# Squares and sums of the second mixer's norm, moved between the gate slabs of the per-layer embedding

## The reference

```python
for i in range(DEPTH):
    xn = _rms(h, norm_mix[i])
    ...
    h = h + mix.astype(h.dtype)
    h = h + _swiglu(_rms(h, norm_ffn[i]), w_ffn_gate[i], w_ffn_up[i], w_ffn_down[i])
    gate = jax.nn.sigmoid(_rms(h, norm_ple[i]) @ w_ple_gate[i])
    h = h + gate * (p[i] @ w_ple_proj[i])
```

## Time and profile before

| | us |
|---|---|
| median of 3 runs | 2720.02 |
| lowest, highest | 2715.08, 2721.79 |
| the profiled execution | 2719.05 |
| its span | 2716.8 |
| mean granted clock of TensorE | 0.956 of full |

### The profile page before, as it was taken

How to read it: one execution, slowest core, us unless ns; L and a number is a source line. 1 busy time by engine, 2 the same in 40 slices (tenths; PEclk the granted TensorE clock), 3 DMA queues, 4 the chain that set the end, 5 groups by cost and what they waited for, 6 DMA issues and landing times.

```text
span 2716.8 us, 40339 instructions
## 1 busy us (share of the span) xinstructions
PE 2558.7 (94%) x15853; PEld 2183.0 (80%) x15853; DVE 1369.3 (50%) x2136; ACT 1164.1 (43%) x1836; POOL 22.6 (1%) x35
## 2 busy tenths in 40 slices
PE   6999999998999999999999879999889998869998
PEld 4777787875777788777887748998779997848998
DVE  4332334995423233422333575555776666476665
ACT  3332223464433322433222365544565554455554
POOL 0000000000000000000000000000000001000000
PEclk7999999999999999999999898998999998689999
DMA  7444532200344432444322303554335554303553
GB/s 280 182 162 177 199 141 83 103 16 31 139 183 158 184 109 102 149 166 179 122 101 93 124 1 115 180 185 174 109 110 191 180 193 148 129 1 105 180 189 146
DMA packets 52723, 374.85 MB, mean 138 GB/s; under 512 B 5822, under 2 KB 7034, under 8 KB 8736
## 3 DMA queue, kind: packets, MB, share of 16 engines
q1 hardware_dynamic: 50288, 360.73, 36.4%
q0 software_dynamic: 1920, 12.27, 1.3%
q10 hardware_dynamic: 432, 0.73, 0.1%
HBM read 372.55 MB, written 7.39 MB: 140 GB/s over the span
## 4 chain that ended last, share of the span: by engine, by line
PE 87%; DVE 7%; ACT 3%; issue 1%; DMA 1%; SPq 0%; ACTq 0%; DVEq 0%
PE acc L1728 27%; PE acc L1729 26%; PE acc L1730 26%; PE bank L1803 3%; ACT sc L1121 1%; PE bank L1830 1%; DVE sc L1663 1%; DMA ada_raw<-in_slabs 1%; DVE sc L1634 1%; DVE wlo L1208 1%; DVE prod L577 1%; PE Mod L1813 0%; ACT whi L739 0%; PE bank L1851 0%; DVE stt L1656 0%
## 5 line engine op out<-in xcount | busy, mean ns | idle before, releaser
L1208 DVE TENSOR_TENSOR wlo<-raw,whi 128x1024 fp32r<-128x1024 f32 x538 | 651.2, 1223 | 943.0 <-ACT whi L739 942.5
L739 ACT ACTIVATE whi<-raw 128x1024 fp32r<-128x1024 f32 x538 | 559.5, 1055 | 990.0 <-PE acc L1730 929.2
L1728 PE MATMUL acc<-hhi,whi 128*128 128x256 f32 (+1 forms) x2800 | 945.6, 338 | 24.7 <-DVE hlo L1292 11.5
L1729 PE MATMUL acc<-hlo,whi 128*128 128x256 f32 (+1 forms) x2800 | 934.4, 334 | 0.0
L1730 PE MATMUL acc<-hhi,wlo 128*128 128x256 f32 (+1 forms) x2800 | 933.9, 334 | 0.0
L1728 PEld LDWEIGHTS acc<-hhi,whi 128*128 128x128 f32 x2800 | 538.0, 192 | 107.6 <-issue 54.3
L1730 PEld LDWEIGHTS acc<-hhi,wlo 128*128 128x128 f32 x2800 | 537.9, 192 | 50.6
L1729 PEld LDWEIGHTS acc<-hlo,whi 128*128 128x128 f32 x2800 | 538.2, 192 | 48.8 <-issue 0.2
L1728 PE MATMUL acc<-ghi,whi 128*128 128x512 f32 (+1 forms) x1056 | 357.3, 338 | 0.0
L1729 PE MATMUL acc<-glo,whi 128*128 128x512 f32 (+1 forms) x1056 | 357.2, 338 | 0.0
L1730 PE MATMUL acc<-ghi,wlo 128*128 128x512 f32 (+1 forms) x1056 | 357.2, 338 | 0.0
(11 more groups left out here) (261 smaller groups left out, 2370.5 us busy)
## 6 DMA issues: line engine op xcount, KB each, us to landing
raw<-in_slabs SPq DMA_DIRECT2D x333, 1024.0 KB, 4.8
ada_raw<-in_slabs SPq DMA_DIRECT2D x8, 1024.0 KB, 23.2
skew_dram<-lines_dram POOLq DMA_DIRECT2D x1, 6144.0 KB, 24.9
bt<-skew_dram POOLq DMA_DIRECT2D x4, 1024.0 KB, 7.1
x<-in_x_in SPq DMA_DIRECT2D x1, 2048.0 KB, 17.7
out<-x SPq DMA_DIRECT2D x1, 1024.0 KB, 4.8
rope<-in_rope POOLq DMA_DIRECT2D x1, 512.0 KB, 4.4
mask<-in_mask POOLq DMA_DIRECT2D x1, 512.0 KB, 5.3
```

The source lines that it names most:

```text
L739: nc.scalar.activation(whi[:, n % 2, cols], raw_of(n, cols), ACT.Copy).then_inc(ready, 1)
L1208: nc.vector.tensor_tensor(wlo[:, n % 2, cols], raw_of(n, cols), whi[:, n % 2, cols].bitcast(F32), ALU.subtract).then_inc(low, 1)
L1728: nc.tensor.matmul(out, w[0], xx[0], start=first, stop=False)
L1729: nc.tensor.matmul(out, w[0], xx[1], start=False, stop=False)
```

## The change

`sq8` is a new buffer for the squares of all eight tiles. In `plegate` of layer 0, ScalarE squares a pair of tiles (128x512 in one instruction) behind the sigmoid of the next slab, and pair 3 behind the table load. TensorE sums pair `c - 1` behind gate slab `c`, and pair 3 in the norm. The eight squares of the norm and their waits fall away. Each one-column sum stays as it was: two matmuls a tile, sixteen in all.

```diff
--- before.py
+++ after.py
@@ plan, make_plan @@
     for i, norm in enumerate(st):
+        if norm.kind == "norm" and st[i - 1].kind == "plegate":
+            st[i - 1].next_norm, norm.carried = norm, True
         if norm.kind == "norm" and not norm.late:
...
@@ plan_with_counts @@
         elif st.kind == "plegate":
             at["ple"] += 4
+            at["sq"] += 4 if st.next_norm else 0
...
             st.summed = st.kind == "norm" and before in ("down", "pw2", "wo", "ada")
+            st.summed |= st.carried
             at["sq"] += 0 if st.summed else DT
...
+        with ExitStack() as pl:
+            sq8 = sb("sq8", [P, DT, S], F32, pl)
...
@@ ScalarE @@
             def plegate(st):
+
+                def pair_squares(c):
+                    act.wait_ge(ple_added, st.ple0 + c + 1)
+                    nc.scalar.activation(sq8[:, 2 * c:2 * c + 2, :], x[:, 2 * c:2 * c + 2, 0:S], ACT.Square)\
+                        .then_inc(sq_ready, 1)
+
                 for c in range(4):
                     m = st.m0 + c
                     g = gate_sb[:, :, (c % 2) * S:(c % 2 + 1) * S]
                     act.wait_ge(acc_free[m % 2], freed(m))
                     nc.scalar.activation(g, g, ACT.Sigmoid).then_inc(ple_gate, 1)
+                    if st.next_norm and c:
+                        pair_squares(c - 1)
                     hi(st.n0 + c + 2)
+                if st.next_norm:
+                    preload(ACT.Sqrt)
+                    pair_squares(3)
...
@@ TensorE @@
+            def pair_sums(st, c):
+
+                pe.wait_ge(sq_ready, st.sq0 - 3 + c)
+                for t in range(2):
+                    ins = token_sums(st, sq8, 2 * c + t, c == 0 and t == 0, c == 3 and t == 1)
+                return ins
+
             def turned_sums(st):
 
+                if st.carried:
+                    pair_sums(st, 3).then_inc(sum_done, 1)
+                    return
                 pe.wait_ge(sq_added, st.add0 + 1)
...
             def plegate(st):
                 for c in range(4):
                     slab_there(st.n0 + c)
                     set_free(st.m0 + c)
                     tiles_of(st.n0 + c, st.m0 + c, (hhi, hlo), S, paced=None if c else st).then_inc(slab_used, 1)
+                    if st.next_norm and c:
+                        pair_sums(st.next_norm, c - 1)
```

More of the change, by code:

```diff
@@ L132, in __init__ @@
         self.late, self.feeds, self.norm, self.both, self.direct = False, None, None, False, False
+        self.next_norm, self.carried = None, False
 def ffn_stages(layer, tokens, ada=0, mod=None):
```

## The result

| | before | changed |
|---|---|---|
| median of 22 runs, us | 2721.18 | 2725.59 |
| lowest to highest | 2715.08 to 2724.24 | 2719.41 to 2728.47 |
| ratio to before | | 1.0017 (1.0010 to 1.0024) |
| the profiled execution | 2719.05 | 2723.76 |

The account below looks back on a forecast made before the run. TensorE, busy 94% of the span, was taken as the bound. Stalls 6.0 less 4.5 won gave 1.5 us, plus 1.6 for the clock: 3.1 on 2719.05, plus 0.97 to the median, 2723.1 us, range 2716.5 to 2729.0.

Parts of the forecast that it names:

- one fall of the clock: In the two stalls between gate slabs, TensorE's clock drops to half once, costing 1.6 us; chance 0.40.
- rival (a): Neither stall between gate slabs moves the clock; only 1.5 us are added, 2721.5 us; chance 0.25.
- rival (b): Both stalls between gate slabs let the clock fall: 1.5 + 3.2 to 4.9 us, 2724.7 to 2726.4; chance 0.23.
- same: Whole-program time within about 0.3% (8.2 us) of before, between 2711.9 and 2728.2 us; chance 0.93.
- Sum one: Path behind slab 3: eight squares out, two larger in, so the root starts 4.5 us earlier.
- Sum two: Behind slabs 1 and 2 TensorE waits for a square, then sums: 3.0 us a stall, 6.0 us in all.
- Sum three: Clock's answer to the two stalls: one fall taken at 1.6 us, with zero and two falls as ends.
- 1.15 us pause: Pause in the trace of before, followed by clock 1.00; lower bound for a stall's clock cost, zero.
- 2.60 us pause: Pause in the trace of before, ended at 1958.08, followed by clock 0.50 for 3.3 us; upper bound, 1.4 us.
- Rival (c): Clock falls in the first stall and stays down until the root: 11.8 us more, 2731.8; chance 0.04.
- Rival (d): No stalls between slabs, the square being done before TensorE asks: 4.5 us won, 2715.5; chance 0.04.
- costed at nothing: Effects priced at zero around the gate slabs: ScalarE's weight split 0.52 us later, unchanged sums count, table loads and queue orders.

Follow-up runs that it names:

- e4: Changed kernel with sixteen dense matmuls of 256 columns behind slabs 1 and 2, ahead of the waiting sums; slabs 8.88 us, ratio to before 1.0008.
- e1: Changed kernel with ScalarE squaring pair c-1 ahead of slab c's sigmoid, sums still between slabs; ratio to before 0.9991.
- e2: Changed kernel with all four sets of TensorE's sums behind slab 3, squares still behind the sigmoids; ratio to before 0.9987.
- e10: e2 with TensorE's wait for the square left behind slabs 1 and 2, without sums there; slabs 9.45 and 8.00 us, one run.
- e9: e4 with eight dense matmuls in place of sixteen in each stall; slabs 10.37 and 10.36 us, one run.
- e8: e3 with thirty matmuls into an unread PSUM bank around pair 3's sums and behind the spreading of the root's reciprocal; ratio to before 0.9957.
- e3: e5 with the last weight slab's split moved out of the chain, behind the root and the norm; ratio to before 0.9974.
- e5: Changed kernel with the edits of e1 and e2 together: squares ahead of the sigmoids, all sums behind slab 3; ratio to before 0.9976.

## Why the prediction was right

The mechanism of the loss and two of the three sums were right; the case it bet on, one fall of the clock, was not the one that came. The range held that case, rival (a) and rival (b) alike, and 0.93 of the chances were on "same", so the number alone could not tell them apart: that it came near is in part luck. Of the 2.5 us between 2723.1 and 2725.59, 1.2 belong to the base (the kernel before has 2721.18 as the median of 22 runs, 2720.02 of three) and 1.3 to the change.

**Sum one**, 4.5 us off the path: 4.31 measured. The square took its 0.52 and 0.61 us; the last sums and the root took 2.04 us behind the square, where 1.78 had been set, so 0.2 us less were won than forecast.

**Sum two**, 3.0 us a stall: 3.04 in the changed kernel, 3.12 with the clock held (e4). The mechanism, a square behind the sigmoid that waits for the slab it was meant to be covered by, is shown by e1 and e2, which remove the wait each from its own side.

**Sum three** is the term that was mis-sized. The prediction took one fall at 1.6 us; both stalls were answered, in both profiles, at 1.57 each. So rival (b) came true, without its slower sums: 1.5 + 3.2 = 4.7, and 4.91 were found at the root. Two steps led there. "Whether a pause is answered also depends on when it comes" was right of the quiet (e10: one of two), but the 0.90 us of one-column sums were only said not to hold the clock up, and not added to the quiet. With them even 1.0 us of quiet was answered twice (e9), shorter than the 1.15 us pause that served as the lower bound.

The prediction also said that the trace of before has no pair of quiet and one-column work between dense slabs, and took the 2.60 us pause as the upper bound. A nearer row stood in that trace, at an earlier norm, behind dense work that ended at 1662.08:

```profile
1661.91 0.95 PE L1830 MATMUL bank<-const,prod 128*128 128x1 f32 x8
1663.16 1.05 PE L1830 MATMUL bank<-const,gate_sb 128*128 128x1 f32 x8 [0.30 <-ACT gate_sb L853]
1664.95 1.22 PE L1851 MATMUL bank<-const,rs_tok 128*128 128x128 f32 x4 [0.73 <-DVE rs_tok L1234]
```

```profile
1664.00:1665.00 1.00, 0.27 (x3) 0.99 0.55 229
1665.00:1666.00 1.00, 1.00 (x4) 0.50 0.00 0
```

The clock fell there although no pause was above 0.73 us: what stood between the dense work and the fall was one-column sums and two short pauses. Read beside the 2.60 us pause, this row speaks for the sums counting with the quiet, and so for two falls.

The trace agrees with the price of a fall, 1.57 us against 1.6, and not with rival (a). By the rule of the Trainium skill, "TensorE: Matmul & The Clock Gate", section "Why this matters for your kernels", idle gaps of this length leave the clock alone. The runs differ: it fell behind every one of the changed kernel's pauses of 1.96 us with the sums behind them, and in e10 behind one of two pauses of 1.97 us with nothing behind them.

Rival (c) did not occur; the clock was back inside each slab. Rival (d) is what e1 builds, and the prediction priced it wrongly: it gave it the whole 4.5 us and forgot that the sums between the slabs hold TensorE 0.9 us each even without a wait. e1 won 3.05 us at the root, 0.5 of them by pair 2's earlier square. What was costed at nothing held: no gate slab waited for its weights in any of these kernels.

## What to carry to other kernels

Work placed behind the next slab is covered by that slab only if its producer stands, on the producer's own engine, ahead of everything that waits for the same slab. Here moving either side of the pair removed the loss of 4.6 us: by the profiles the root came 3.05 us (squares moved) or 4.31 us (sums moved) earlier than in the kernel before, by the whole runs 0.9991 (0.9980 to 1.0001) and 0.9987 (0.9977 to 0.9998). If TensorE has idle time later on the same path, sums belong there, and dense filler behind them is worth trying where a dense stretch follows.

## What the runs showed of the hardware

A fall of TensorE's clock was bought by less than expected: 1.01 us of quiet with 0.9 us of one-column matmuls behind it, twice in two (e9), while 0.88 us of the same matmuls alone did not (e1, two places between slabs). A run of 24 one-column records without a pause let it fall in two kernels of three: in e8 TensorE ran them from 2248.74 on, and the clock went from 1.00 to 0.50 between 2250.5 and 2251; in e3 from 2246.53 on, and it fell between 2248.5 and 2249; in e5 they ended at 1.00. So a TensorE that the profile calls busy can still lose its clock. In e8 it came back by 2258.00, while the twenty matmuls behind the spreading ran.
